# Where the matmul operands of four FFNs start inside a 128-byte block

## The reference

```
x = diff_pool_layer(x)                     # stage L0: differential attention and pooling
x = conv_glu_ffn(x, f_w_up[0], ...)        # F0
x = swa_layer(x)                           # L1: sliding-window attention
x = conv_glu_ffn(x, f_w_up[1], ...)        # F1
x = x + 0.5 * swiglu_ffn(rms_norm(x), w13, w2)   # F2
x = x + mixer(rms_norm(x))                 # MIX: convolution module and forgetting attention
x = x + 0.5 * swiglu_ffn(rms_norm(x), w13, w2)   # F3
return rms_norm(x)
```

## Time and profile before

| what | us |
|---|---|
| median of 3 runs | 1047.77 (1047.63 to 1049.26) |
| profiled execution, its own time | 1045.93 |
| its span, first to last instruction | 1044.1 |
| PE busy | 1015.0 (97%) |
| PE weight loads busy | 908.8 (87%) |
| DVE busy | 747.4 (72%) |
| ACT busy | 626.1 (60%) |
| POOL busy | 357.3 (34%) |

### The profile page before, as it was taken

How to read it: one execution, slowest core, us unless ns; L and a number is a source line. 1 busy time by engine, 2 the same in 40 slices (tenths; PEclk the granted TensorE clock), 3 DMA queues, 4 the chain that set the end, 5 groups by cost and what they waited for, 6 DMA issues and landing times.

```text
span 1044.1 us, 15953 instructions
## 1 busy us (share of the span) xinstructions
PE 1015.0 (97%) x6502; PEld 908.8 (87%) x6502; DVE 747.4 (72%) x1010; ACT 626.1 (60%) x881; POOL 357.3 (34%) x189
## 2 busy tenths in 40 slices
PE   7999999999999899999999999999999899999997
PEld 7899988888977798888888888888999698888885
DVE  5876999874558789998638766654799787666532
ACT  6776777663455568776536654544669866455531
POOL 1062277530100024766102545510176323555300
PEclk9999999999999999999999999999999999999999
DMA  9633675646332345655553665556342157565341
GB/s 346 217 127 126 234 260 190 212 146 240 122 121 81 113 151 202 225 179 203 198 197 128 242 199 170 196 201 219 124 163 81 57 190 259 182 202 194 134 155 40
DMA packets 27143, 183.45 MB, mean 176 GB/s; under 512 B 3008, under 2 KB 3136, under 8 KB 5824
## 3 DMA queue, kind: packets, MB, share of 16 engines
q1 hardware_dynamic: 26496, 181.40, 49.2%
q10 hardware_dynamic: 576, 1.05, 0.3%
HBM read 181.39 MB, written 1.05 MB: 175 GB/s over the span
## 4 chain that ended last, share of the span: by engine, by line
PE 83%; DVE 11%; ACT 4%; issue 2%; DMA 0%; POOL 0%; DVEq 0%; ACTq 0%; POOLq 0%
PE psum L330 82%; DVE wlo L1548 3%; DVE Pb L1679 1%; DVE psum L1554 1%; ACT whi L1021 1%; DVE bias L1554 1%; ACT Pb L1155 1%; DVE Y L1554 1%; DVE gain_x L1554 1%; DVE Pb L1551 0%; DVE QK L1554 0%; DMA gain_x<-in_x 0%; DVE G L1548 0%; DVE Cb L1554 0%; POOL Y L2223 0%
## 5 line engine op out<-in xcount | busy, mean ns | idle before, releaser
L330 PE MATMUL psum<-G,whi 128*128 128x512 f32 (+1 forms) x1840 | 548.3, 359 | 7.6 <-DVE wlo L1548 7.5
L1548 DVE TENSOR_TENSOR wlo<-raw,whi 128x2048 fp32r<-128x2048 f32 (+1 forms) x170 | 388.6, 2299 | 184.8 <-ACT whi L1021 184.8
L330 PE MATMUL psum<-G,wlo 128*128 128x256 f32 x1560 | 439.9, 282 | 0.0
L1021 ACT ACTIVATE whi<-raw 128x2048 fp32r<-128x2048 f32 (+1 forms) x170 | 315.8, 1869 | 153.9 <-PE psum L330 140.5
L330 PEld LDWEIGHTS psum<-G,whi 128*128 128x128 f32 x1840 | 327.5, 189 | 61.7 <-DVE G L1554 6.3
L330 PEld LDWEIGHTS psum<-G,wlo 128*128 128x128 f32 x1560 | 295.5, 189 | 0.1
L330 PE MATMUL psum<-A,whi 128*128 128x512 f32 (+1 forms) x784 | 228.6, 354 | 0.0
L2223 POOL TENSOR_TENSOR A<-Ab,A 128x512 fp32r<-128x512 f32 x44 | 141.6, 3218 | 130.8 <-ACT A L1021 130.8
L330 PE MATMUL psum<-A,wlo 128*128 128x256 f32 x656 | 184.6, 281 | 0.0
L330 PEld LDWEIGHTS psum<-A,whi 128*128 128x128 f32 x784 | 138.2, 188 | 20.9
L2223 POOL TENSOR_TENSOR Ab<-Cb 128x512 f32<-128x512 f32 x44 | 113.7, 2583 | 105.6 <-ACT Cb L1064 105.1
(11 more groups left out here) (190 smaller groups left out, 1058.2 us busy)
## 6 DMA issues: line engine op xcount, KB each, us to landing
raw<-in_wst SPq DMA_DIRECT2D x165, 1024.0 KB, 5.0
bias<-in_bias_c SPq DMA_DIRECT2D x1, 2048.0 KB, 9.5
raw<-in_wst SPq DMA_DIRECT2D x3, 512.0 KB, 8.1
raw<-in_wst ACTq DMA_DIRECT2D x4, 256.0 KB, 6.5
out<-bias SPq DMA_DIRECT2D x4, 256.0 KB, 2.1
gain_x<-in_x SPq DMA_DIRECT2D x3, 256.0 KB, 6.8
bias<-in_bias_a SPq DMA_DIRECT2D x1, 512.0 KB, 8.5
bias<-in_invcnt SPq DMA_DIRECT2D x1, 512.0 KB, 8.4
```

Of the source, the lines that this page charges most:

```text
L330: return pe.matmul(o, a, b, start=start, stop=stop, skip_group_check=True)
L1021: return act.activation(o, i, ACT.Copy)
L1548: return dve.tensor_tensor(o, a, b, op)
```

## The change

`G2` becomes `G2room` and `A2` becomes `A2room`, each with 32 elements (128 bytes) to spare. Two tables give for each stage at which element of the room its operand starts: `normed(ph)` for `G2`, `activations(ph)` for `A2`, `unscaled(ph)` for `E2`. `off_64` goes, so that `A2room`, `wextra` and `Hb` start at a multiple of 128; `off_M` puts `Mhi`, `Mlo` and what follows them back to 32. `Cb` and `Ab` come to 64. The order of instructions, their waits and their shapes are the same on every engine; only addresses differ.

Distances of the operands, in bytes:

| stage | normed input, before and after | activations (and `E2`), before and after | role |
|---|---|---|---|
| L0, L1, MIX | 32, 32 | - | as before |
| F0 | 32, 64 | 32, 64 | moving |
| F1 | 32, 96 | 32, 96 | moving |
| F2 | 32, 16 | 32, 16 | moving |
| F3 | 32, 32 | 32, 0 | input moving, activations stationary |
| `wextra` (MIX) | - | 32, 0 | stationary weights |

The other weights stay at distance 0 throughout.

```diff
+def phase_of(i):
+
+    return max(ph for ph in FIRST if FIRST[ph] <= i)
+
+G_AT = {L0: 0, F0: 8, L1: 0, F1: 16, F2: 28, MIX: 0, F3: 0}
+A_AT = {F0: 16, F1: 24, F2: 4, F3: 0}
...
-        G2 = sb("G2", [P, DT, 2, S], F32R)
-        Ghi, Glo = G2[:, :, 0, :], G2[:, :, 1, :]
+
+        G2room = sb("G2room", [P, DT * 2 * S + 32], F32R)
+
+        def normed(ph):
+            a = G2room[:, G_AT[ph]:G_AT[ph] + DT * 2 * S]
+            return a.rearrange("p (t a s) -> p t a s", t=DT, a=2)
+
...
-        sb("off_64", [P, 8])
-
         with ExitStack() as reg:
-            A2 = sb("A2", [P, FT, 2, S], F32R, reg)
-            Ahi, Alo = A2[:, :, 0, :], A2[:, :, 1, :]
-
-            E2 = A2[:, FT - DT:FT, :, :]
+
+            A2room = sb("A2room", [P, FT * 2 * S + 32], F32R, reg)
...
+        def activations(ph):
+            a = A2room[:, A_AT[ph]:A_AT[ph] + FT * 2 * S].rearrange("p (t a s) -> p t a s", t=FT, a=2)
+            return a[:, :, 0, :], a[:, :, 1, :]
+
+        def unscaled(ph):
+
+
+            if ph not in (F0, F1):
+                return normed(ph)
+            a = A2room[:, A_AT[ph] + (FT - DT) * 2 * S:A_AT[ph] + FT * 2 * S]
+            return a.rearrange("p (t a s) -> p t a s", t=DT, a=2)
+
...
         with ExitStack() as reg:
+            sb("off_M", [P, 8], F32, reg)
             Mhi = sb("Mhi", [P, DT, S], F32R, reg)
...
             def wide(b, i, h, ph=None, conv=None):
...
                 h3, l3 = weights(i, DT)
+                G = normed(phase_of(i))
...
-                        mm(bank[b + n], h3[:, k, ws], G2[:, k, :, :].rearrange("p a s -> p (a s)"), k == 0, False)
-                        last = mm(bank[b + n][:, 0:S], l3[:, k, ws], G2[:, k, 0, :], False, k == DT - 1)
+                        mm(bank[b + n], h3[:, k, ws], G[:, k, :, :].rearrange("p a s -> p (a s)"), k == 0, False)
+                        last = mm(bank[b + n][:, 0:S], l3[:, k, ws], G[:, k, 0, :], False, k == DT - 1)
...
+                A = A2room[:, A_AT[ph]:A_AT[ph] + FT * 2 * S].rearrange("p (t c) -> p t c", t=FT)
...
-                        add_rows(ph, c0 + 22 + j, j, Ahi, Alo, j == 0, j == FP - 1, tiles_ready, out_free, FP, True)
+                        add_rows(ph, c0 + 22 + j, j, *activations(ph), j == 0, j == FP - 1, tiles_ready, out_free, FP, True)
```

More of the change, by code:

```diff
@@ L338, in weights, with half @@
                 return (v.rearrange("p (k n) -> p k n", k=k) for v in halves(i))
-            def half(b, i, h, ph=None, G=G2):
+            def half(b, i, h, ph=None, G=None):
                 h3, l3 = weights(i, DT)
+                if G is None:
+                    G = normed(phase_of(i))
                 if h == 0 and i > 1:
@@ L360, in first_chunk @@
                 h3, l3 = weights(0, DT)
+                G = normed(L0)
                 for j in range(4):
@@ L367, in first_chunk, with wide @@
                                 pe.wait_ge(s_lo, j + 1)
-                            last = three(bank[b][:, n * S:n * S + S], h3[:, k, ws], l3[:, k, ws], Ghi[:, k, :], Glo[:, k, :],
+                            last = three(bank[b][:, n * S:n * S + S], h3[:, k, ws], l3[:, k, ws], G[:, k, 0, :], G[:, k, 1, :],
                                          k == 0 and n == 0, k == DT - 1)
                 last.then_inc(s_used, 1)
-            def wide(b, i, h, ph=None, normed=None):
+            def wide(b, i, h, ph=None, conv=None):
                 h3, l3 = weights(i, DT)
+                G = normed(phase_of(i))
                 if h == 0:
@@ L382, in wide @@
                             pe.wait_ge(s_glo, 8 * ph + k + 1)
-                        if n == 0 and normed is not None:
-                            pe.wait_ge(s_nlo, 2 * normed + k // 4 + 1)
+                        if n == 0 and conv is not None:
+                            pe.wait_ge(s_nlo, 2 * conv + k // 4 + 1)
                         ws = slice(n * P, n * P + P)
-                        mm(bank[b + n], h3[:, k, ws], G2[:, k, :, :].rearrange("p a s -> p (a s)"), k == 0, False)
-                        last = mm(bank[b + n][:, 0:S], l3[:, k, ws], G2[:, k, 0, :], False, k == DT - 1)
+                        mm(bank[b + n], h3[:, k, ws], G[:, k, :, :].rearrange("p a s -> p (a s)"), k == 0, False)
+                        last = mm(bank[b + n][:, 0:S], l3[:, k, ws], G[:, k, 0, :], False, k == DT - 1)
                 if h == 1:
@@ L397, in tokens_first @@
                         xs = slice(t * P, t * P + P)
-                        last = three(bank[b][:, t * S:t * S + S], Ghi[:, k, xs], Glo[:, k, xs], h3[:, k, :], l3[:, k, :],
+                        last = three(bank[b][:, t * S:t * S + S], G[:, k, 0, xs], G[:, k, 1, xs], h3[:, k, :], l3[:, k, :],
                                      k == 0, k == DT - 1)
@@ L487, in up_conv @@
                         pe.wait_ge(s_rt, ph + 1)
-                    half(at(ph, 2 + e), c0 + 2 + e, 0, None, E2)
-                    half(at(ph, 2 + e), c0 + 2 + e, 1, None, E2)
+                    half(at(ph, 2 + e), c0 + 2 + e, 0, None, unscaled(ph))
+                    half(at(ph, 2 + e), c0 + 2 + e, 1, None, unscaled(ph))
                 for p in range(NARROW, FP):
@@ L769, in l1 @@
                 h3, l3 = weights(c0 + 2, DT)
+                G = normed(L1)
                 pe.wait_ge(s_lo, low_done(c0 + 2))
                 for k in range(DT):
-                    three(bank[0][:, 0:S], h3[:, k, 0:P], l3[:, k, 0:P], Ghi[:, k, :], Glo[:, k, :], k == 0, k == DT - 1)
+                    three(bank[0][:, 0:S], h3[:, k, 0:P], l3[:, k, 0:P], G[:, k, 0, :], G[:, k, 1, :], k == 0, k == DT - 1)
                 for t in range(2):
@@ L775, in l1 @@
                         xs = slice(t * P, t * P + P)
-                        last = three(bank[0][:, S + t * P:S + t * P + P], Ghi[:, k, xs], Glo[:, k, xs],
+                        last = three(bank[0][:, S + t * P:S + t * P + P], G[:, k, 0, xs], G[:, k, 1, xs],
                                      h3[:, k, P:S], l3[:, k, P:S], k == 0, k == DT - 1)
@@ L877, in forget @@
                     h3, l3 = weights(c0 + 4, DT)
+                    G = normed(MIX)
                     pe.wait_ge(s_lo, low_done(c0 + 4))
                     for k in range(DT):
-                        last = three(bank[2][:, 0:S], h3[:, k, :], l3[:, k, :], Ghi[:, k, :], Glo[:, k, :], k == 0, k == DT - 1)
+                        last = three(bank[2][:, 0:S], h3[:, k, :], l3[:, k, :], G[:, k, 0, :], G[:, k, 1, :], k == 0, k == DT - 1)
                     last.then_inc(s_used, 1)
@@ L1037, in residual @@
                         for n in (2 * j_, 2 * j_ + 1):
-                            act.activation((E2 if nxt in (F0, F1) else G2)[:, n, 0, :], X[:, n, :], ACT.Identity,
+                            act.activation(unscaled(nxt)[:, n, 0, :], X[:, n, :], ACT.Identity,
                                            scale=col(GAIN[nxt], n)).then_inc(s_ghi, 1)
@@ L1173, in first @@
                     act.wait_ge(s_xin[j], 16)
-                    act.activation(Ghi[:, 2 * j, :], X[:, 2 * j, :], ACT.Copy, scale=gain_x[:, 2 * j:2 * j + 1]).then_inc(s_ghi, 1)
+                    act.activation(normed(L0)[:, 2 * j, 0, :], X[:, 2 * j, :], ACT.Copy, scale=gain_x[:, 2 * j:2 * j + 1]).then_inc(s_ghi, 1)
                     act.wait_ge(s_w0[j], 16)
                     copy(whi[:, 0, ws], raw[:, 0, ws]).then_inc(s_hi, 1)
-                    act.activation(Ghi[:, 2 * j + 1, :], X[:, 2 * j + 1, :], ACT.Copy, scale=gain_x[:, 2 * j + 1:2 * j + 2]).then_inc(s_ghi, 1)
+                    act.activation(normed(L0)[:, 2 * j + 1, 0, :], X[:, 2 * j + 1, :], ACT.Copy, scale=gain_x[:, 2 * j + 1:2 * j + 2]).then_inc(s_ghi, 1)
                 def square(j, o):
@@ L2244, in a_low @@
                     pool.wait_ge(s_ahi, FP * n + p + 1)
-                    TT(Alo[:, 2 * p:2 * p + 2, :], Ab[:, p % 2, :, :], f(Ahi[:, 2 * p:2 * p + 2, :]), ALU.subtract).then_inc(s_alo, 1)
+                    h, l = (a[:, 2 * p:2 * p + 2, :] for a in activations(ph))
+                    TT(l, Ab[:, p % 2, :, :], f(h), ALU.subtract).then_inc(s_alo, 1)
                 def gate_up(p):
```

18 lines of the change are left out of this document (9 added, 9 removed).

## The result

The changed kernel is slower by a factor of 1.0041, 95% interval 1.003 to 1.0052: 1051.39 us median of 9 runs against 1046.62 us of 9 runs of the kernel before. The ratio makes 4.3 us, with 3.1 to 5.4 as the interval; the two medians lie 4.8 apart. The forecast was 3.0 us more, between 1.6 and 5.7. (Before's median over nine runs is 1.15 us under that of the three shown ahead, so the ratio is compared and not the absolute time.)

What follows compares the result with a forecast made beforehand. PE's matmul pace was taken to bound the FFNs. Terms of 2.8 (F0), 0 (F1), 0 (F2), 0.4 (F3) and -0.2 (wextra) made 3.0 us, giving 1050.8 us from 1047.77; its own range was 1049.4 to 1053.5, overall 1045.4 to 1055.0.

Steps and rivals of the forecast that it cites:

- What bounds: Whole kernel: PE is 83% of the chain of waits; FFN time is number of matmuls times pace, which alone can move.
- F0, wide pairs: F0's 464 wide matmul pairs, moving operand at 64: 5.0 ns more each (3.5 to 6.6), 2.3 us in all.
- The rule behind it: PE matmuls: moving and stationary operands at equal distance modulo 64 cost, 3.3 ns a matmul; 32 apart is cheap.
- F0, narrow blocks: F0's 64 blocks of three narrow matmuls: 7.4 ns more each (4.8 to 9.9), 0.5 us in all.
- F1: F1, moving operand at 96, taken as 32 apart modulo 64: no change, bounded by 0.1 us gain and 1.3 us loss.
- F2: F2, moving operand at 16, not the equal case: no change; 2.6 us loss or 3.5 us gain considered as extremes.
- F3 and MIX: F3's down product, both operands at 0: 0.4 us more (0 to 0.9); MIX's 72 wextra matmuls: 0.2 us less.
- The other engines: ACT, DVE and POOL reading and writing at new distances: no cost; open first writes 7.7 us at the very most.
- No effect: First rival, all matmuls: distance from 128 means nothing; 1047.8 us, or 1047.6 if wextra gains; chance 0.31.
- the gain on a multiple: Second rival: starts inside a 64-byte unit cost, so F0 gains 1.9 us, F3's down product 0.9; 1044.8 us; chance 0.14.
- The third: Rival for F0, F1, F2: every place but 32 past is worse; 6.7 us more, 1054.5 us; chance 0.17.
- Lines and ports: Skill's 16-byte memory lines and independent PE read ports, cited for the no-change rival: multiples of 16 should behave alike.

Runs made afterwards that it cites:

- the best of these runs: Kernel before with F3's stationary activations at the weights' place modulo 256 and wextra 160 before MIX's input; 0.9965 of the kernel before, 1044.09 against 1048.25 us.

## Why the prediction was right, point by point

**What bounds.** Right. PE is busy all through the wide chunks, before and after, and time moved only with the pace.

**F0, wide pairs.** That the pace would move, and upwards, was right; the size was too small: I priced a pair at 5.0 ns more, between 3.5 and 6.6, and it is 6.7, the upper end: 464 pairs make 3.1 us instead of 2.3. The end that added's 3.3 ns to each member was the better one, but for no good reason, as the next point shows.

**The rule behind it.** "Equal distance modulo 64 costs" is half right. That the difference counts and not the place is shown by moving weights and activations together. That the dear case is equality modulo 64 fell: equal places gave 346.7 ns in F0 with the weights at 32, while 48, 80, 96 and 112, none of them equal, cost 3.4 to 6.7 ns. 32 is one of few good differences rather than the ordinary case. So F0's price came out by luck: it was taken from rows at a difference of 0 and of 224 (the earlier trace rows and F3's pace), and F0's operands lie at 64 and 192, which no row had shown and which happen to be dear.

**F0, narrow blocks.** Priced at 0.5 us, it was 0.1. The first piece rose by 1.1 ns a matmul; the second ran at 340.2 ns for three, faster than before, and gained nothing. Nothing waits for its end, as the chain of waits of the changed kernel shows: from 106.89 us on it goes through ACT's and DVE's norm to the weights' low part.

```profile
106.91 0.49 ACT Rt L1129
...
107.87 3.26 DVE bias L1583 x8
...
116.18 2.21 DVE wlo L1577
118.40 0.25 issue
118.64 11.42 PE psum L351 x63
```

**F1.** Priced at 0, it cost 1.0 us. This is the step that failed: 96 was taken as 32 modulo 64. The bound of 1.3 us held by chance, for it came from the two levels of the earlier trace rows, and the cost is 3.5 ns a pair in the up product.

**F2.** Priced at 0, and its stage is equal within 0.01 us over 528 pairs. The reason given, that 16 isn't the equal case, is none: 48 and 112 aren't either, and cost.

**F3 and MIX.** The down product was priced 0.4 us dearer and became 1.0 ns a matmul cheaper, 0.3 us. The sign was wrong: no row of before had a 512-column matmul at another difference. `wextra` gained about 0.1 us of the 0.2 forecast, 2.5 ns a matmul in its first 24, and 1 ns in its second. MIX as a whole is 0.3 us longer in the profile, but with the clock at half for 3.4 us more, so its sum can't show what the addresses did.

**The other engines.** Right to cost them at nothing: with F0 put back and `Hb`, `Cb` and `Ab` at the new places F0 is at 184.57 us against 184.49.

**The rivals.** No effect is ruled out by F0's pairs; the gain on a multiple too. The third, every place but 32 dearer, was right for 64 and 96 and wrong for 16. It had F0 at 5.0 and F1 at 3.5 ns, and F1's part happened in the up product. The total, 4.3 us, lies between the forecast's 3.0 and this rival's 6.7, nearer to the forecast. That is in part luck too: F1 (+1.0), F0 (+0.4) and L0 (up to +0.5) came out dearer than priced, and F3 (-0.7) cheaper.

**Lines and ports.** By the Trainium skill's lines of 16 bytes (SBUF — State Buffer, Specifications) nothing should have changed among multiples of 16; the trace doesn't agree, with 346.7 ns at 16 and 353.3 at 64. The same page of the Trainium skill (Who interferes with whom) has PE's two read ports as independent. The runs show the pace of a matmul to depend on the difference of the two operands' addresses, 350.1 ns a pair at 96 and 346.7 at 32; whether this arises at the ports or in the memory behind them, no run tells. Why some differences are good and others not stays open.

## What to carry to other kernels

Where float32r matmuls run back to back as here, the place of the moving operand relative to the stationary one, in bytes modulo 256, is a tuning knob. From good to dear it was worth 1% to 3% of the pace of these wide pairs, free of any instruction; the kernel before already had most operands at a good difference, and the best of these runs gained under 2 us on it, 0.2%. Measure the pace from start to start over some hundred matmuls for each form apart, and at more than one place of the program, because at some differences the same stream runs at either of two levels. Moving one operand doesn't tell whether its place counts or its distance from the other: move both together as the control.

## What the runs showed of the hardware that I had not expected

- At the full clock and a difference of 32 a narrow matmul takes 116.7 ns for 256 columns, 280 cycles of 2.4 GHz, and a wide pair 346.7 ns, 832 cycles for 768 columns. In the 3.4 us at half the clock (1.2 GHz) 256 columns take 213.3 ns, which is 256 cycles: four matmuls from 371.27 to 372.12 us, 0.21 us each. In these traces the extra cycles are there only at the full clock.

```profile
371.27 0.41 PE L351 MATMUL psum<-Mhi,whi 128*128 128x256 f32 x1
...
372.12 0.41 PE L351 MATMUL psum<-Mlo,whi 128*128 128x256 f32 x1
```

- The commonest levels are multiples of 8 cycles of 2.4 GHz for 768 columns: 340.0, 346.7, 350.0 and 353.3 ns are 816, 832, 840 and 848 cycles, 48, 64, 72 and 80 too many.
- No product of an FFN was seen to change its level while it ran without a pause: with weights and moving activations both at 32, wide pairs stay at 353.3 ns from 398.6 to 573.4 us, and come out of the pause there at 346.7. A new product takes a level of its own without a pause: with all four FFNs at 96, the up products of F0 and F1 both run at 350.0 ns and the down products behind them at 353.3 and 346.7. What decides which isn't shown.
